# Adding the bias and the mask of an attention with an identity product on TensorE

## The reference

```python
# first block, both layers: 8 heads of width 64 (256 tokens are one block, so nothing but the own block is seen)
s_own = einsum('bhqd,bhld->bhql', q, k) * scale
s_own = where(k_pos <= q_pos, s_own, NEG_INF)        # causal mask
p = softmax(s_own); o = einsum('bhql,bhld->bhqd', p, v)

# second block, layers 0 and 3: differential attention, 8 heads, each with two halves c of width 64
logits = einsum('bqhcd,bkhcd->bhcqk', q, k) * scale
logits = logits + bias[head, bucket(dist)]           # relative bias, the same for both halves
logits = where(dist >= 0, logits, -inf)
p = softmax(logits)
attn = p[:, :, 0] - lam * p[:, :, 1]; o = einsum('bhqk,bkhd->bqhd', attn, v)
```

## Time and profile before

| | us |
|---|---|
| Median of 3 runs | 3086.26 (3085.7 to 3089.04) |
| The profiled execution's own time | 3090.16 |
| its span in the profile | 3088.4 |
| PE busy in it | 2873.8 (93%) |
| DVE busy | 1951.1 (63%) |
| ACT busy | 1370.3 (44%) |
| mean granted TensorE clock | 0.956 of full speed |

### The profile page before, as it was taken

How to read it: one execution, slowest core, us unless ns; L and a number is a source line. 1 busy time by engine, 2 the same in 40 slices (tenths; PEclk the granted TensorE clock), 3 DMA queues, 4 the chain that set the end, 5 groups by cost and what they waited for, 6 DMA issues and landing times.

```text
span 3088.4 us, 50830 instructions
## 1 busy us (share of the span) xinstructions
PE 2873.8 (93%) x21087; PEld 2713.7 (88%) x21087; DVE 1951.1 (63%) x2702; ACT 1370.3 (44%) x1640; POOL 0.7 (0%) x5
## 2 busy tenths in 40 slices
PE   6899989999998899969999978999989999969998
PEld 6899869999997799959899977989989899959898
DVE  3887767768759555555466664566655566555665
ACT  2334434344353444544444514444444545444443
POOL 0000000000000000000000000000000000000000
PEclk7999979999998999989999998999999999979999
DMA  7987507969862155624255613344644355614453
GB/s 212 301 284 241 170 22 250 297 221 298 281 204 96 55 192 180 224 71 151 90 197 189 202 60 108 125 161 171 212 151 150 131 197 192 203 45 134 153 174 109
DMA packets 458800, 533.03 MB, mean 173 GB/s; under 512 B 9879, under 2 KB 435081, under 8 KB 458633
## 3 DMA queue, kind: packets, MB, share of 16 engines
q1 hardware_dynamic: 458633, 530.76, 52.2%
HBM read 528.10 MB, written 2.62 MB: 172 GB/s over the span
## 4 chain that ended last, share of the span: by engine, by line
PE 84%; DVE 9%; ACT 3%; issue 2%; DMA 1%; SPq 1%; DVEq 0%; ACTq 0%
PE ps L1876 15%; PE ps L1711 12%; PE ps L1861 11%; PE ps L2155 8%; PE ps L1693 6%; PE ps L1695 6%; PE ps L1694 6%; PE ps L1862 5%; PE ps L1741 2%; PE ps L1739 2%; PE ps L1740 2%; PE ps L1945 2%; PE ps L1916 2%; DVE work L1436 1%; DMA work<-in_ada_w 1%
## 5 line engine op out<-in xcount | busy, mean ns | idle before, releaser
L1063 DVE TENSOR_TENSOR wlo<-raw,whi 128x2048 fp32r<-128x2048 f32 (+1 forms) x514 | 976.9, 1919 | 475.6 <-ACT whi L720 475.5
L720 ACT ACTIVATE whi<-raw 128x2048 fp32r<-128x2048 f32 (+1 forms) x514 | 824.9, 1611 | 399.9 <-PE ps L1695 125.0
L1861 PE MATMUL ps<-parts_f,whi 128*128 128x512 f32 x1408 | 504.9, 402 | 9.9 <-issue 9.9
L1862 PE MATMUL ps<-parts_f,wlo 128*128 128x256 f32 x1408 | 397.7, 282 | 0.0
L1693 PE MATMUL ps<-hhi,whi 128*128 128x256 f32 x1360 | 388.9, 286 | 2.7 <-DVE wlo L1063 1.5
L1694 PE MATMUL ps<-hlo,whi 128*128 128x256 f32 x1360 | 386.3, 284 | 0.0
L1695 PE MATMUL ps<-hhi,wlo 128*128 128x256 f32 x1360 | 386.3, 284 | 0.0
L1876 PE MATMUL ps<-ghi,whi 128*128 128x256 f32 x1280 | 363.2, 284 | 2.4 <-DVE wlo L1063 2.4
L1876 PE MATMUL ps<-glo,whi 128*128 128x256 f32 x1280 | 363.1, 284 | 0.0
L1876 PE MATMUL ps<-ghi,wlo 128*128 128x256 f32 x1280 | 363.0, 284 | 0.0
L1861 PEld LDWEIGHTS ps<-parts_f,whi 128*128 128x128 f32 x1408 | 267.2, 190 | 75.3 <-issue 11.3
(11 more groups left out here) (257 smaller groups left out, 4902.3 us busy)
## 6 DMA issues: line engine op xcount, KB each, us to landing
raw<-in_ffn_w_in SPq DMA_DIRECT2D x88, 1024.0 KB, 8.0
raw<-in_ffn_w_gu SPq DMA_DIRECT2D x88, 1024.0 KB, 5.0
work<-in_ada_w SPq DMA_DIRECT2D x72, 1024.0 KB, 8.7
raw<-in_ffn_w_out SPq DMA_DIRECT2D x88, 512.0 KB, 5.7
raw<-in_ffn_w_down SPq DMA_DIRECT2D x88, 512.0 KB, 5.6
raw<-in_ca_w_kv SPq DMA_DIRECT2D x32, 1024.0 KB, 5.4
raw<-in_mix_w_in SPq DMA_DIRECT2D x24, 1024.0 KB, 5.7
raw<-in_da_w_in SPq DMA_DIRECT2D x24, 1024.0 KB, 5.3
```

What stands on the lines that cost most here:

```text
L720: f(whi[:, s, 0:size], raw[:, s, 0:size], ACT.Copy).then_inc(hi_done[s], 1)
L1063: tt(wlo[:, s, 0:size], raw[:, s, 0:size], whi[:, s, 0:size].bitcast(F32), ALU.subtract).then_inc(lo_done[s], 1)
L1861: mm(ps[:, banks[m], :], th[:, k, c], parts_f[:, :, k, :], start=k == 0, stop=False)
L1862: o = mm(ps[:, banks[m], 0:S], tl[:, k, c], fhi[:, k, :], start=False, stop=k == KT - 1)
```

## The change

PE now adds mask or bias itself: behind each score product a second product with the identity matrix (128 deep, all rows of the array) adds the table to the same PSUM columns. DVE's adds and the semaphore `masked` go. DVE takes maxima from PSUM, and ACT reads the exponentials' input from PSUM and writes SBUF. The waits move with that: PE waits for `exped` (the exponentials of head j-2) before it writes a score bank, DVE waits for `exped` too, and ACT waits for `turned_mm` before it writes the SBUF rows. The wait for the bias table moves from DVE to PE.

```diff
 # ACT, mix1 (diff likewise, with four parts of two banks)
                         act.wait_ge(q["maxed"], J + 1)
-                        s = m_s[:, j % 2, :]
-                        exp_rows(J, (s[:, 0:P], s[:, P:384]), (s[:, 0:P], s[:, P:384]), stat[:, j % 2, 0:2],
+                        if J > 1:
+                            act.wait_ge(q["turned_mm"], J - 1)
+                        d, s = ps[:, (4, 0)[j % 2], :], m_s[:, j % 2, :]
+                        exp_rows(J, (d[:, 0:P], d[:, P:384]), (s[:, 0:P], s[:, P:384]), stat[:, j % 2, 0:2],
                                  stat[:, j % 2, 4:6])
 # DVE, mix1
-                            dve.wait_ge(q["turned_mm"], J - 1)
-                        s = m_s[:, j % 2, :]
-                        tt(s, ps[:, (4, 0)[j % 2], 0:384], causal, ALU.add).then_inc(q["masked"], 1)
-                        dve.wait_ge(q["masked"], st.masked + j + 1)
-                        v.tensor_reduce(stat[:, j % 2, 0:1], s[:, 0:P], AX.X, ALU.max, negate=True)
-                        v.tensor_reduce(stat[:, j % 2, 1:2], s[:, P:384], AX.X, ALU.max, negate=True)\
+                            dve.wait_ge(q["exped"], J - 1)
+                        d = ps[:, (4, 0)[j % 2], :]
+                        v.tensor_reduce(stat[:, j % 2, 0:1], d[:, 0:P], AX.X, ALU.max, negate=True)
+                        v.tensor_reduce(stat[:, j % 2, 1:2], d[:, P:384], AX.X, ALU.max, negate=True)\
 # DVE, diff
-                dve.wait_ge(q["aux_in"], (16, 64)[st.n])
...
-                        dve.wait_ge(q["turned_mm"], J - 1)
-                        s = d_s[:, j % 2]
-                        for c0, c1, b0 in ((0, P, P), (P, 384, 0)):
-                            m = tt(s[:, :, c0:c1], ps[:, b:b + 2, c0:c1],
-                                   d_bias[:, j:j + 1, b0:b0 + c1 - c0].broadcast_to([P, 2, c1 - c0]), ALU.add)
-                        m.then_inc(q["masked"], 1)
-                        dve.wait_ge(q["masked"], st.masked + j + 1)
-                        v.tensor_reduce(stat[:, j % 2, 0:2], s[:, :, 0:P], AX.X, ALU.max, negate=True)
-                        v.tensor_reduce(stat[:, j % 2, 2:4], s[:, :, P:384], AX.X, ALU.max, negate=True)\
+                        dve.wait_ge(q["exped"], J - 1)
+                        v.tensor_reduce(stat[:, j % 2, 0:2], ps[:, b:b + 2, 0:P], AX.X, ALU.max, negate=True)
+                        v.tensor_reduce(stat[:, j % 2, 2:4], ps[:, b:b + 2, P:384], AX.X, ALU.max, negate=True)\
 # PE, mix1
-                            pe.wait_ge(q["masked"], st.masked + j - 1)
+                            pe.wait_ge(q["exped"], st.heads + j - 1)
                         d = ps[:, (4, 0)[j % 2], :]
-                        mm(d[:, 0:P], mq[rows_, tile, 0:P], mk[rows_, tile, 0:P], start=True, stop=True)
-                        mm(d[:, P:384], mq[rows_, tile, P:S], mk[rows_, tile, :], start=True, stop=True)\
-                            .then_inc(q["scores_mm"], 1)
+                        mm(d[:, 0:P], mq[rows_, tile, 0:P], mk[rows_, tile, 0:P], start=True, stop=False)
+                        mm(d[:, 0:P], ident, causal[:, 0:P], start=False, stop=True)
+                        mm(d[:, P:384], mq[rows_, tile, P:S], mk[rows_, tile, :], start=True, stop=False)
+                        mm(d[:, P:384], ident, causal[:, P:384], start=False, stop=True).then_inc(q["scores_mm"], 1)
 # PE, diff
+                pe.wait_ge(q["aux_in"], (16, 64)[st.n])
...
-                        pe.wait_ge(q["masked"], st.masked + j - 1)
+                        pe.wait_ge(q["exped"], st.heads + j - 1)
...
-                            mm(d[:, 0:P], dq[rows_, j, 0:P], dk[rows_, j, 0:P], start=True, stop=True)
-                            o = mm(d[:, P:384], dq[rows_, j, P:S], dk[rows_, j, :], start=True, stop=True)
+                            mm(d[:, 0:P], dq[rows_, j, 0:P], dk[rows_, j, 0:P], start=True, stop=False)
+                            mm(d[:, 0:P], ident, d_bias[:, j, P:S], start=False, stop=True)
+                            mm(d[:, P:384], dq[rows_, j, P:S], dk[rows_, j, :], start=True, stop=False)
+                            o = mm(d[:, P:384], ident, d_bias[:, j, :], start=False, stop=True)
```

More of the change, by code:

```diff
@@ L136, in __init__ @@
                  pos=None, reads=None, modnorm=None, units=None, src=None, name=None, l=None, mixer=None,
-                 uses=None, ada=None, last=None, gn=None, heads=None, masked=None, pairs=None, tree=None,
+                 uses=None, ada=None, last=None, gn=None, heads=None, pairs=None, tree=None,
                  rope=None, j=None, layer=None, n=None, h=None, early=False, late=None, add=None, defer=None, turn=None, then=None):
@@ L144, in __init__ @@
         self.ada, self.last, self.gn, self.heads = ada, last, gn, heads
-        self.masked, self.pairs, self.tree, self.rope = masked, pairs, tree, rope
+        self.pairs, self.tree, self.rope = pairs, tree, rope
         self.j, self.layer, self.n, self.h, self.early, self.late = j, layer, n, h, early, late
@@ L354, in build @@
         stages = plan.stages
-        tally = dict.fromkeys("add defer norm modnorm ffn gn heads masked pairs tree rope project out diff".split(), 0)
+        tally = dict.fromkeys("add defer norm modnorm ffn gn heads pairs tree rope project out diff".split(), 0)
         def take(name, n=1):
@@ L406, in build @@
             stages.append(Stage(kind="mix1", l=l, units=units, last=units[-1], gn=take("gn", 5), heads=take("heads", 8),
-                                masked=take("masked", 8), pairs=take("pairs", 4), tree=take("tree"),
+                                pairs=take("pairs", 4), tree=take("tree"),
                                 rope=take("rope", 4)))
@@ L425, in build @@
                 stages.append(Stage(kind="diff", j=j, layer=i, units=units, last=units[-1], n=take("diff"),
-                                    heads=take("heads", 8), masked=take("masked", 8), pairs=take("pairs", 4),
+                                    heads=take("heads", 8), pairs=take("pairs", 4),
                                     gn=take("gn", 4)))
@@ L955, in diff @@
                         act.wait_ge(q["maxed"], J + 1)
-                        s = d_s[:, j % 2]
-                        src = [s[:, c, r] for r in (slice(0, P), slice(P, 384)) for c in range(2)]
-                        exp_rows(J, src, src, stat[:, j % 2, 0:4], stat[:, j % 2, 4:8])
+                        act.wait_ge(q["turned_mm"], J - 1)
+                        s, b = d_s[:, j % 2], (4, 0)[j % 2]
+                        parts = [(c, r) for r in (slice(0, P), slice(P, 384)) for c in range(2)]
+                        exp_rows(J, [ps[:, b + c, r] for c, r in parts], [s[:, c, r] for c, r in parts],
+                                 stat[:, j % 2, 0:4], stat[:, j % 2, 4:8])
                     if j >= 5 and j % 2:
@@ L1976, in mix1 @@
                 pe.wait_ge(q["rope_done"], st.rope + 4)
+                causal = const("causal")
                 def part(h):
```

6 lines of the change are left out of this document (2 added, 4 removed).

## The result

| kernel | median of its runs | lowest, highest | runs |
|---|---|---|---|
| before, same chip | 3087.65 us | 3085.7, 3094.26 | 4 |
| after | 3108.97 us | 3104.8, 3111.0 | 4 |

The change makes the kernel slower: ratio 1.0065, with an interval of 1.0053 to 1.0078, or 21.3 us between the medians. The forecast was 3111 and slower. Its total is right. How that total is made up is half wrong: the forecast had 12 us in `diff` and 13 in `mix1`, and the traces show 26 and 0.

A forecast was written before the change was run, and what follows sets the result against it. PE was to replace DVE as the bound in `diff`; `diff` plus 12 and `mix1` plus 13 made 25 on 3090.2, so 3115, or 3111 for the median. Eight-in-ten range 3095 to 3142.

The forecast's parts named there:

- The bound in `diff` changes from DVE to PE: In `diff` at the full clock, PE needs 5.0 us a head, DVE's chain without adds and its wait 2.6.
- The terms of a head: PE's costs per `diff` head: 1.28 scores, 1.28 identity, four round trips of 0.37, 0.32 transposes, 0.64 values: 5.0 us.
- the forecast's walk: `diff`, first scores to second norm's sum at the full clock: 43.5 us, plus 3.0 and plus 1.9 over before.
- The overlap of the halves: In `diff`, score halves no longer run side by side: a head's scores stream 1.28 us instead of 0.64.
- The clock in `diff`: The 2.6 us wait at the norm's sum can cost heads 6 and 7 the full clock; half taken, plus 3.6 a stage.
- The last term of that walk: In `diff`, the hand-over from head 7's scores to the second norm's sum, 3.65 us.
- `mix1`: plus 13 forecast: Both `mix1` stages: 9.2 us added in the first, 6.7 in the second, less 2.7 for the clock.
- I take half, 2.7: First `mix1` stage: a busier PE may get some of the second stage's 5.4 us clock advantage; half is taken.
- The first rival: The clock pays: PE keeps the full clock, `diff` plus 5, `mix1` plus 8.5, total 3100; chance 0.22.
- A whole stage locked at the half clock: Rival: a `diff` stage stays at 9.0 us a head; one stage 3137, both 3162; chance 0.17.
- Free mode changes: Rival: switches cost nothing in the new order, a `diff` head takes 3.9 us, total 3081; chance 0.07.
- The third rival: Faster: halves side by side and switch hidden, a `diff` head costs PE 3.25 us, total 3070; chance 0.04.

The follow-up runs named there:

- The pair of experiments with equal mode changes: After's `diff` order changed to two round trips between row modes a head: halves one after the other, 3087.01 us; halves side by side, 3075.03 us.
- only-`diff` kernel: The change made in the `diff` stages alone, `mix1` as in before with its mask add on DVE: 3112.24 us, ratio 1.008 to before.
- the sum moved: After, with PE's first norm sum in `diff` put behind head 6's scores: 3092.37 us over ten runs, ratio 1.0019 to before.
- the grouped order: After, with all four score products of a `diff` head first, then its four identity products: 3071.79 us; same idea in `mix1` too: 3067.67 us.
- two round trips: After, with each half of a `diff` head doing its scores, then its tables, halves not side by side: 3087.01 us, ratio 0.9991 to before.

## Why the prediction was right, and where it was not

**The bound in `diff` changes from DVE to PE: right.** DVE's 2.57 us of wait for L2056 shows it in the row, and the runs with other orders show it in their times: fewer mode changes minus 22 us (of which the clock has a part), the halves together minus 12, with DVE's program the same in all of them.

**The terms of a head: right, nearly all a little low.** Round trip 0.41 measured against 0.37 (0.58 against 0.50 at the half clock), the scores of a head 4.08 against 3.9, head 5.16 against 5.0 (9.41 against 9.0), DVE's busy time minus 25.9 against 25, wait at the norm's sum 2.46 against 2.6. From the first scores to the first sum both stages take 30.8 us; the forecast's walk had 7.9 + 4.4 + 15.0 + 2.6 = 29.9.

**The overlap of the halves: right.** Forecast at 0.64 us a head. The pair of experiments with equal mode changes isolates it: a head at the full clock takes 4.38 us in the one and 3.74 in the other, 0.64 less. By the medians it is 12 us over 16 heads, 0.75 each, partly at the half clock. The Trainium skill says both things in words (TensorEngine Tiling (Array Packing), Key Properties: a change of tiling mode drains the engine, tiles of one mode run in parallel), and the runs agree with both.

**The clock in `diff`: right place, wrong size. This is the first step that failed.** The forecast said that the wait at the norm's sum "can cost it for heads 6 and 7, some 3.6 each. I take half: plus 3.6 a stage". From the first sum to the second are 24.7 and 20.5 us, where the forecast's terms at the full clock give 0.95 + 5.0 + 4.0 + 3.65 = 13.6. So it was 11.1 and 6.9 us instead of 3.6 twice, 10.8 too little. The first stage lost both heads to the half clock and the second one of them; in the two stages of the only-`diff` kernel it was one each. That the clock falls was given a chance of a half, and it fell behind this wait in all four profiled stages with after's order. Its price was low too. In the first stage the sum took 1.0 us more than its full-clock term, head 6 4.4 more and head 7's scores 3.4 more: 8.8, where the forecast had 7.2 for both heads. In the second stage the sum and head 6 took 4.9 more.

**The last term of that walk: 3.65 us from head 7's scores to the second sum.** The forecast took it from head 5, whose maxima are DVE's next work. Head 7's maxima wait behind the subtraction L1582, and the term measured 5.93 and 5.58 us, 2.3 and 1.9 more, the second with PE at the full clock. These are the rest of the 11.1 and 6.9, and they are not of the clock. That the second sum has the longer wait could be read in the kernel before: 4.67 us against 3.83.

With the sum moved and the first wait gone, both heads kept the full clock in the profiled run; four of that kernel's ten runs were as slow as if only the wait had gone. With the 0.9 a stage of the walk's first part, the forecast's 12 became 3.0 + 0.9 + 11.1 = 15.0 and 1.9 + 0.9 + 6.9 = 9.7 up to the second sum, and 15.4 and 10.5 for the whole stages. (The 1.9 is 43.5 less 41.7, which is 1.8.)

**`mix1`: plus 13 forecast, 0 measured. This is the second step that failed**, and it failed in the term "I take half, 2.7" for the clock, and in the walk, which priced heads 3 to 6 at the half clock. Three profiles of the unchanged stages sum to 112.0, 112.1 and 109.8 us, five with the change in after's order to between 111.7 and 112.2. The first rival had the mechanism right here, the clock rose to full at head 3 and stayed for 37.6 us, nearly to the stage's end, but its plus 8.5 was too high as well. The time at the half clock fell by 23.3 us in the first stage and by 7.8 in the second. If all of it gave back half its length, an estimate that is high where PE waits anyway, that is 11.7 and 3.9, against the walk's 9.2 and 6.7 without the clock: minus 2.5 and plus 2.8, where minus 2.5 and plus 2.5 were measured. So the term of 2.7 should have been nearly 16. What of it is DVE's relief and what the clock was not separated. The row that I held against it, 402 to 420 at the half clock with PE busy 16.1 of 18.0, was of a PE with other products in it; after had 16.57 of 17.0 busy at the half clock and then the full one. I had read that row as a property of the stage, and it was one of the old order of work. The forecast had named its own sign here: it would be wrong "if the clock in the four stages leaves 0.64 to 0.76 by much". The four stages had 0.84, 0.83, 0.77 and 0.87. It had them longer by 6, 7, 7 and 6 us, and they were by -2.5, 2.5, 15.4 and 10.5.

**Two errors of opposite sign.** 26 for 12, and 0 for 13, sum to 26 against 25. Then the rest of the span was 11 us shorter in the one profile against the other, while the medians differ by 21.3. That the forecast of the total is so near is luck. The sign and the mechanism in `diff` are not: the only-`diff` kernel shows the loss again without the `mix1` part, and the grouped order takes it away with the same products and the same DVE program.

**The other rivals.** A whole stage locked at the half clock did not occur: 32.8 and 17.8 us of half clock in stages of 70 and 66. (The first of them is nearly half of its stage, though, which is some of the way to that rival.) Free mode changes and side-by-side halves did not occur in this order. The third rival's condition, the halves side by side, is just what the grouped order makes true, and that kernel is at 3071.8, where the rival had 3070; a switch is not hidden there either (2.28 us for 0.64 + 1.28 of passes), so the agreement is of the total only.

## What to carry to other kernels

Work that moves to PE as an identity product is cheap in passes and dear in mode changes: put products of 64 rows together and those of 128 rows together, with the tiles that can run side by side next to each other. In the grouped kernels only the first product into a bank starts it; whether it must be so no run here shows. Read the granted clock on both sides of a wait on PE: by one profile each, a stop of 2.5 us in front of a long stretch of PE work cost 8 to 13 us with the half clock behind it, and issuing the next head's scores first removed that, though, by the times, in six runs of ten only. The order behind the stop matters too: after the same wait of 2.46 us the half clock lasted 10.2 to 20.5 us in after's order, 6.8 with two round trips and 3.4 in the grouped order. A stage at the half clock may get the full one with other products in it, so price such work at both levels and keep both ends.

## What was unexpected

- **More work on PE, less time.** `mix1` with one grouped identity product per head is 53.5 us long, twice in each of two profiles, and without any 56.5, with 14.4 and 39.4 us at the half clock. Dead products in before's `mix1` cost 2.8 us of stage time for 17 us or more of work, part of which went into PE's waits. What about the products brings the full clock was not isolated.
- **Stages that repeat, and stages that don't.** `mix1` in after's order took 55.8 to 56.1 us in all ten stages profiled, with 18.2 to 18.6 us at the half clock. Unchanged it took 53.1 to 59.0 us, with 22.5 to 48.7. The change took the spread away and left the mean (112.0 us for two stages against 109.8 to 112.1).
- **PSUM as a source cost nothing.** DVE's maxima take 0.68 us for 512 columns from PSUM and from SBUF alike.
